# Attention gates of the two layers as 256-column groups, high and low part of the input in one moving operand

## What is computed

```python
h = rms_norm(x, norm_g[l]) * (1.0 + scale) + shift
z = h @ w_in[l]
q_lat, kv_lat, k_rope, mla_gate, conv_in, conv_gate = jnp.split(z, splits, axis=-1)
...
attn = causal_block_attention(q, k, v).reshape(b, s, D_MLA)
mla_out = attn * jax.nn.silu(mla_gate)          # mla_gate: 256 tokens x 1024
u = u_val * jax.nn.sigmoid(u_gate)
u = causal_depthwise_conv(u, dw_w[l], dw_b[l])  # 31 taps, 1024 channels
u = jax.nn.silu(layer_norm(u, conv_ln_g[l], conv_ln_b[l]))
conv_out = (u @ w_pw[l] + b_pw[l]) * jax.nn.silu(conv_gate)
y = jnp.concatenate([mla_out, conv_out], axis=-1) @ w_out[l]
x = x + gate * y
```

## Time and profile before

| | |
|---|---|
| median of 3 runs | 1965.21 us (1964.45 to 1965.22) |
| the profiled execution's own time | 1965.23 us |
| its span, first to last instruction | 1963.4 us |
| PE busy | 1939.5 us (99%) |
| DVE busy | 1525.6 us (78%) |
| ACT busy | 1069.1 us (54%) |
| granted TensorE clock | 1.00 |

### The profile page before, as it was taken

The page is one execution under the profiler, slowest core; times in us unless marked ns, Lnnn a source line. Parts: engine busy times, 40 slices in busy tenths (PEclk is TensorE's granted clock), DMA queues, the critical chain, the costliest instruction groups (busy, mean ns, idle before and its releaser), DMA issues.

```text
span 1963.4 us, 27925 instructions
## 1 busy us (share of the span) xinstructions
PE 1939.5 (99%) x11546; PEld 1682.9 (86%) x11546; DVE 1525.6 (78%) x2092; ACT 1069.1 (54%) x1545; POOL 0.2 (0%) x4
## 2 busy tenths in 40 slices
PE   7999999999999999999999999999999999999999
PEld 6888888888888888888888889999888899998887
DVE  6587776868887777788877567999966669999764
ACT  5474766455654443555534475554764556456742
POOL 0000000000000000000000000000000000000000
PEclk9999999999999999999999999999999999999999
DMA  7443445948988889999898644544455454454453
GB/s 283 153 165 125 140 149 201 358 134 297 342 328 334 332 329 331 330 327 344 331 336 336 240 135 155 190 165 141 161 191 181 158 176 175 151 171 134 172 195 123
DMA packets 63982, 442.59 MB, mean 225 GB/s; under 512 B 7248, under 2 KB 7536, under 8 KB 12400
## 3 DMA queue, kind: packets, MB, share of 16 engines
q1 hardware_dynamic: 61920, 434.30, 61.8%
q10 hardware_dynamic: 1936, 6.51, 0.9%
HBM read 438.67 MB, written 2.11 MB: 224 GB/s over the span
## 4 chain that ended last, share of the span: by engine, by line
PE 95%; DVE 2%; ACT 2%; DMA 0%; issue 0%; ACTq 0%; DVEq 0%
PE PS L630 22%; PE PS L632 11%; PE PS L509 11%; PE PS L511 11%; PE PS L510 11%; PE PS L578 7%; PE PS L579 7%; PE PS L580 7%; PE PS L501 6%; DVE WL L1082 1%; DVE Y L1124 0%; PE PS L657 0%; ACT WH L1918 0%; DMA X<-in_x 0%; ACT S L1981 0%
## 5 line engine op out<-in xcount | busy, mean ns | idle before, releaser
L1918 ACT ACTIVATE WH<-RAW 128x1024 fp32r<-128x1024 f32 (+1 forms) x636 | 664.0, 1049 | 755.1 <-PE PS L511 291.0
L1082 DVE TENSOR_TENSOR WL<-RAW,WH 128x1024 fp32r<-128x1024 f32 (+1 forms) x636 | 766.7, 1209 | 376.3 <-ACT WH L1918 375.2
L630 PE MATMUL PS<-HT,WH 128*128 128x512 f32 x1912 | 678.5, 398 | 0.0
L632 PE MATMUL PS<-HT,WL 128*128 128x256 f32 x1912 | 535.8, 280 | 0.0
L630 PEld LDWEIGHTS PS<-HT,WH 128*128 128x128 f32 x1912 | 358.6, 188 | 88.7 <-issue 7.2
L632 PEld LDWEIGHTS PS<-HT,WL 128*128 128x128 f32 x1912 | 361.3, 189 | 0.1
L578 PE MATMUL PS<-HT,WH 128*128 128x256 f32 x1008 | 291.2, 289 | 2.3 <-DVE HT L1078 1.1
L579 PE MATMUL PS<-HT,WH 128*128 128x256 f32 x1008 | 285.5, 283 | 0.0
L580 PE MATMUL PS<-HT,WL 128*128 128x256 f32 x1008 | 285.4, 283 | 0.0
L1091 DVE SCALAR_TENSOR_TENSOR RAW<-RAW,CB 128x2048 f32<-128x2048 f32 x96 | 219.3, 2284 | 0.0
L578 PEld LDWEIGHTS PS<-HT,WH 128*128 128x128 f32 x1008 | 193.4, 192 | 12.4 <-issue 7.8
(11 more groups left out here) (317 smaller groups left out, 2025.7 us busy)
## 6 DMA issues: line engine op xcount, KB each, us to landing
RAW<-in_w_in SPq DMA_DIRECT2D x112, 1024.0 KB, 4.8
RAW<-in_ada_w SPq DMA_DIRECT2D x96, 1024.0 KB, 6.2
RAW<-in_w_up SPq DMA_DIRECT2D x64, 1024.0 KB, 6.0
RAW<-in_w_down SPq DMA_DIRECT2D x64, 1024.0 KB, 5.9
RAW<-in_w_out SPq DMA_DIRECT2D x48, 1024.0 KB, 4.8
RAW<-in_w_pw SPq DMA_DIRECT2D x8, 1024.0 KB, 4.7
RAW<-in_w_in SPq DMA_DIRECT2D x8, 768.0 KB, 4.1
RAW<-in_w_q_up SPq DMA_DIRECT2D x6, 1024.0 KB, 4.9
```

The source lines that it names most:

```text
L630: e.matmul(bk[i][:, 0:512], wh[:, at], m["HT"][:, kt, :, :].rearrange("p a t -> p (a t)"), start=kt == 0, stop=False, skip_group_check=True)
L632: op = e.matmul(bk[i][:, 0:256], wl[:, at], HTh[:, kt, :], start=False, stop=kt == n.kts - 1, skip_group_check=True)
L1082: e.tensor_tensor(m[f"WL{j % NHL}"][:, 0:nk * w], m[f"RAW{i % NRAW}"][:, k0 * w:(k0 + nk) * w], m[f"WH{j % NHL}"][:, 0:nk * w].bitcast(F32 ...
L1918: e.activation(m[f"WH{j % NHL}"][:, 0:nk * w], m[f"RAW{i % NRAW}"][:, k0 * w:(k0 + nk) * w], ACT.Copy).then_inc(signals["high"], 1)
```

## The change

In both layers the attention gates are projected in four joint groups of 256 columns instead of two groups of 512. They join the conv gates in one list OUT_GATES of eight groups (7 to 14) with one loop on each engine. The count of chunks, of halves, of beats and the bytes stay as they are. The tile MG (Y[:, 0]) takes the attention gates, CG (Y[:, 1]) the conv gates, as before.

```diff
-GLU_VALUES, GLU_GATES, Q_LATENT, KV_LATENT, MLA_GATES, CONV_GATES = ((0, 1), 5), (2, 6), 3, 4, (7, 8), (9, 10, 11, 12)
-LAYER_JOINT = GLU_VALUES[0] + CONV_GATES
+GLU_VALUES, GLU_GATES, Q_LATENT, KV_LATENT, OUT_GATES = ((0, 1), 5), (2, 6), 3, 4, tuple(range(7, 15))
+LAYER_JOINT = GLU_VALUES[0] + OUT_GATES
...
-        "w_in2": (16, [256] * 2 + [512] * 2 + [384] + [512] * 4 + [256] * 4),
+        "w_in2": (16, [256] * 2 + [512] * 2 + [384] + [512] * 2 + [256] * 8),
...
-        for g in MLA_GATES:
-            products(group[f"w_in2_{L}", g], *hidden, h, cols=4)
-        for g in CONV_GATES:
+        for g in OUT_GATES:
             joint_products(group[f"w_in2_{L}", g], h)
...
-                dve.wait_ge(*group[f"w_in2_{L}", MLA_GATES[h // 4]].taken)
+                dve.wait_ge("out_gates", 4 * L + h // 4 + 1)
                 dve.wait_ge("a_pv", 8 * L + h + 1)
                 tt("a_out", MG[:, h, :], values[:, 0:256], MG[:, h, :], ALU.mult)
...
-        for n in [group[f"w_in2_{L}", g] for g in MLA_GATES + CONV_GATES] + [
+        for n in [group[f"w_in2_{L}", g] for g in OUT_GATES] + [
                 group[f"w_out2_{L}", cg, "half"] for cg in range(2)]:
             for j, _ in course.begin(n):
                 if before is not None and j == n.first + 1:
-                    at = 2 * CONV_GATES.index(before)
-                    summed(before, CG[:, at:at + 2, :])
-            before = next((g for g in CONV_GATES if group[f"w_in2_{L}", g] is n), None)
+                    k = OUT_GATES.index(before)
+                    at = 2 * (k % 4)
+                    summed(before, (CG if k >= 4 else MG)[:, at:at + 2, :])
+            before = next((g for g in OUT_GATES if group[f"w_in2_{L}", g] is n), None)
...
-        for k, g in enumerate(MLA_GATES):
-            n = group[f"w_in2_{L}", g]
-            course.group(n)
-            store_T(n, MG[:, 4 * k:4 * k + 4, :], ACT.Silu)
-
-        def gates_done(half):
-
-            act.wait_ge("joint_sum", 2 * joint_index(CONV_GATES[2 * half + 1], L) + 2)
-            part = CG[:, 4 * half:4 * half + 4, :]
-            e.activation(part, part, ACT.Silu).then_inc(signals["cg"], 1)
-
-        for k, g in enumerate(CONV_GATES):
+        def gates_done(k):
+
+            act.wait_ge("joint_sum", 2 * joint_index(OUT_GATES[2 * k + 1], L) + 2)
+            part = (MG, CG)[k // 2][:, 4 * (k % 2):4 * (k % 2) + 4, :]
+            e.activation(part, part, ACT.Silu).then_inc(signals["out_gates"], 1)
+
+        for k, g in enumerate(OUT_GATES):
             n = group[f"w_in2_{L}", g]
             for j, _ in course.begin(n):
-                if k == 2 and j == n.first + 2:
-                    gates_done(0)
-            second_part(n, CG[:, 2 * k:2 * k + 2, :])
+                if k and k % 2 == 0 and j == n.first + 2:
+                    gates_done(k // 2 - 1)
+            second_part(n, (MG, CG)[k // 4][:, 2 * (k % 4):2 * (k % 4) + 2, :])
```

More of the change, by code:

```diff
@@ L294, in weight_course @@
         weights(f"w_q_up_{layer}", range(3))
-        weights(f"w_in2_{layer}", MLA_GATES + CONV_GATES)
+        weights(f"w_in2_{layer}", OUT_GATES)
         for i in range(2):
@@ L344 @@
     "warm mean root rstd xs turned ht_v ht_h ht_l x_sq x_up mix_h mix_l tile0 y_sum y_sq y_gain "
-    "joint_low joint_sum glu cg mix_gates va_mm va score score_in top top_neg soft_exp soft_sink soft_add probs pt_mm pt pv oa att_sq att_part att_ss att_ms att_root att_out "
+    "joint_low joint_sum glu out_gates mix_gates va_mm va score score_in top top_neg soft_exp soft_sink soft_add probs pt_mm pt pv oa att_sq att_part att_ss att_ms att_root att_out "
     "ones_row lb lb_sig r_f r_log r_key r_cum r_last r_att r_diag r_gap r_exp0 r_edge r_cross r_ax "
@@ L1793, in vector_program @@
         UV, UG = m["UV"], m["UG"]
-        CG = Y[:, 1, :].rearrange("p (h t) -> p h t", h=8)
+        MG, CG = (Y[:, i, :].rearrange("p (h t) -> p h t", h=8) for i in range(2))
         def summed(g, part):
@@ L1865, in vector_program @@
             dve.wait_ge("half_done", n.done)
-            dve.wait_ge("cg", 2 * L + 2)
+            dve.wait_ge("out_gates", 4 * L + 4)
             for f in range(4):
@@ L2288, in channel_norm @@
                 act.wait_ge("n_silu", 4 * L + f // 2 + 1)
-                act.wait_ge("half_done", group[f"w_in2_{L}", CONV_GATES[-1]].done)
+                act.wait_ge("half_done", group[f"w_in2_{L}", OUT_GATES[-1]].done)
                 e.activation(HTh[:, 8 + f:10 + f, :], UG[:, f:f + 2, :], ACT.Copy).then_inc(signals["p_h"], 1)
@@ L2630, in scalar_program @@
                 if cg == 0 and j == n.first + 2:
-                    gates_done(1)
+                    gates_done(3)
         course.drain(side, norm)
```

## The result

The changed kernel takes 1967.37 us (median of 20 runs, 1967.13 to 1969.38) against 1964.59 us (20 runs, 1964.33 to 1967.19) of the kernel before on the same chip. The medians are 2.8 us (0.14%) apart. The ratio of the runs is 1.0013, 95% interval 1.0007 to 1.0019: slower, inside the 0.2% that a measurement can hardly tell from no change, yet with an interval that leaves 1 out. Forecast was 1967.7 us, 2.5 more than the profiled execution of the kernel before (1965.23). These 20 runs of the kernel before have a median 0.6 us under the three that the forecast started from, so the difference is the fairer thing to compare: 2.5 forecast, 2.8 measured (2.6 by the ratio).

The account below looks back on a forecast made before the run. DVE, full from the start of the gates to the last tap, was taken as the bound. Per layer 2.64 - 1.48 + 0.10 = 1.26 us; 1965.23 + 2 x 1.26 = 1967.75, stated as 1967.7 us, range 1963.4 to 1969.6.

Parts of the forecast that it names:

- The bound: Start of the gates to last tap: DVE is full, so anything added to it comes out later by its full length.
- PE waits hardly at all today: Hand-overs from DVE to PE in the kernel before: little to spare, 1.48 us at the last taps.
- DVE, added: Four pairs of adds a layer, at steps 5, 9, 13 and 17, before the last tap: 2.64 us a layer.
- The upper end of 0.41 each: Cost of one add standing alone, giving at most 3.28 us a layer for the eight.
- ACT: Two Silu stores replaced by eight copies and two wide Silus, costed at nothing.
- the third rival: Second wide Silu, step 18, delays ACT's cast and so DVE: 1968.1 to 1970.3 us, chance 0.14.
- Followed through: Layer 0 traced step by step: delays at steps 6, 16 and 26, ending 1.26 us late.
- Steps 6, 16 and 26: PE needs the query norm's reciprocal, second head's probabilities, last taps (first matmuls over UG): 0.6, 0.8 to 0.9, 1.26 us late.
- the term for the hand-over: Step 26: time from DVE's result to the waiting engine, taken as 0.10 us, between 0.04 and 0.19.
- PE, removed: Attention gates, 256 fewer matmuls over both layers: saves 0.9 to 1.75 us a layer, 1.75 taken.
- my lower bound: Smallest saving from the removed matmuls, 0.9 us a layer.
- By step 14 PE has gained that back: Step 14: PE has recovered the delay of about 0.6 us from step 6.

Follow-up runs that it names:

- before_more_adds: The kernel before with eight spare DVE adds a layer, a pair at each of steps 5, 9, 13 and 17: 1968.13 us, ratio 1.0013.
- slow12: The changed kernel with SLOW_TURNS 12 instead of 20, moving eight taps a layer ahead of the gates to the latents: 1965.36 us, ratio 1.0001.
- before_slow12: The kernel before with SLOW_TURNS 12 instead of 20: 1964.25 us, ratio 0.9999.
- small_adds: The changed kernel with the attention gates' eight adds a layer cut from 256 to 16 columns (gates then wrong): 1964.8 us, ratio 1.0000.
- norm_later: The changed kernel with the channel norm's strand opened one step later, so PE asks for the last taps later: 1967.54 us, ratio 1.0010.

## Why the prediction was right

**The bound.** "DVE is full from the start of the gates to the last tap, so an add comes out later by its full length": shown, by 0.67, 1.32, 1.99 and 2.64 us behind the four pairs, and by the spare adds: in the kernel before they cost 1.44 a layer, close to the change's own 1.28. "PE waits hardly at all today" holds but for the 0.15 us at step 9.

**DVE, added.** 8 x 0.33 = 2.64: measured 0.67 a pair and 2.64 in all. The upper end of 0.41 each did not occur. Of the three instructions in the earlier trace rows two are adds and the third is the multiply of the attention output (`a_out`), of the same shape and price.

**ACT.** Costed at nothing, and before_more_adds reaches the loss without ACT's new work. The second wide Silu, on which the third rival rested, waits for nothing. The timeline of ACT in the changed kernel, steps 10 and 18 of layer 0:

```profile
1358.63 1.06 ACT L2609 ACTIVATE Y<-Y 128x1024 f32<-128x1024 f32 x1 [1.21 <-DVE Y L1076]
...
1388.31 1.28 ACT L2609 ACT_TABLE_LOAD   x1
1389.61 1.06 ACT L2609 ACTIVATE Y<-Y 128x1024 f32<-128x1024 f32 x1
```

The first one waits 1.21 us for DVE, which I had not foreseen, but ACT then waits 0.90 us for PE before its next cast, so nothing was behind it.

**Followed through.** Steps 6, 16 and 26 were forecast at 0.6, 0.8 to 0.9 and 1.26 us late, and came at 0.62, 0.92 and 1.29. At step 26 the term for the hand-over was taken as 0.10 and is 0.15 (1415.78 to 1415.93). Layer 1 is alike: 1.30 over UG (1826.73 against 1824.99, less the 0.44 by which DVE's splits ahead of its gates are late, 1727.76 against 1727.32).

**PE, removed: the mis-sized term.** I took 1.75 us a layer from the quiet pace of 0.3465, and named 0.9 as the bound by 0.353. What came is half of what I took. The first two halves of the attention gates run at 0.347 us a tile, and save 0.2 us together. Behind the first side strand some halves run at 0.353 (in the changed kernel 1325.07 to 1327.19, six tiles) and some at 0.347 (31 tiles from 1357.9 on). The whole is best read where PE has no listed wait and DVE is relieved in both forms, in slow12 against before_slow12: from the first matmul over SQR to the first head's transposes at step 14 the joint form takes 49.05 us (1324.08 to 1373.13) and the old one 49.68 (1323.89 to 1373.57). That is 0.63, with the first two halves 0.83 in 15 halves and 0.9 in the layer: my lower bound. It did not hurt the forecast, because PE's end is set by the waits at 6, 16 and 26; in a kernel with DVE on time the same slip would have been 0.9 us a layer. It did hurt the expectation for small_adds, which reckoned with 0.11 us a half and drew. The one for slow12 reckoned with 0.05, which is what came, and fell by the waits.

"By step 14 PE has gained that back" was wrong for the same reason, and because the changed kernel too loses some 0.1 us at step 9. From the first matmul over HS to the transposes of the first head at step 14 the changed kernel takes 29.87 us against 30.29 before, so 0.42 of the 0.62 was gained back.

**What hides what.** With the wait of step 26 taken away (norm_later) PE is still 0.9 us late from the wait of step 16, so most of the loss is held by more than one wait; it goes only when DVE's queue ahead of all of them is shorter.

## What to carry to other kernels

Where two engines are both covered, an operation moved from one to the other is not weighed by its length on each but by the slack of the hand-overs behind it: here 1.48 us of slack at the last taps turned 2.64 us of adds into a loss of 1.28 a layer, and 0.9 us of saved matmuls counted for nothing. Find the slack of each hand-over in the timelines first, and look for idle time of the fuller engine in an earlier stretch: moving eight taps to an earlier stretch paid back the whole loss, though only half of their time arrived, since DVE can't run further ahead than ACT's casts let it. The distance between one instruction's starts in two equal layers resolves some 0.15 us here, which 20 runs of 1965 us can't.

## What was not expected of the hardware

**Two paces of one instruction stream.** At a granted clock of 1.00 TensorE runs the tile of the joint form at 0.3467 or at 0.3533 us, for one or two halves at a time among the side strands, and elsewhere for stretches of 100 us and more. In the same work of the first block's MLP, the kernel before takes 0.3533 at 440 to 600 us, where the changed one takes 0.3467 until 480 and 0.3533 from about 500. PE's timeline in the changed kernel, matmuls 15 tiles apart, near 440 and near 560:

```profile
439.30 0.39 PE L630 MATMUL PS<-HT,WH 128*128 128x512 f32 x1
...
444.50 0.39 PE L630 MATMUL PS<-HT,WH 128*128 128x512 f32 x1
```

```profile
559.25 0.40 PE L630 MATMUL PS<-HT,WH 128*128 128x512 f32 x1
...
564.55 0.40 PE L630 MATMUL PS<-HT,WH 128*128 128x512 f32 x1
```

That is 5.20 and 5.30 us for the same 15 tiles. The quicker stretch put the changed kernel's profile some 0.8 us ahead at 500 us, and so it stays up to the attention gates. It does not go with the form of the gates: the first matmul over SQR of layer 0 starts at 1324.65 in the kernel before and at 1323.84 in before_more_adds, which runs the same program up to there; and at 1323.62 in the changed kernel but at 1324.50 in small_adds, which also does. Of the 20 runs of the kernel before, 11 lie from 1964.33 to 1964.61 us and 7 from 1965.19 to 1965.35, as far apart; whether it is the same thing is not shown. What sets the pace was not tested.

**GpSimd beside DVE.** An add of two SBUF tiles of 128x256 takes 0.74 us on GpSimd in four of 12 cases, in which it starts beside DVE instructions with at most one SBUF input, 1.18 in the mean of all 12, and 2.57 at most, beside a split. On DVE the add from PSUM takes 0.33. Taps that overlap a GpSimd add take 0.733 us, the others 0.475.
